# Two transformer-like blocks in one kernel: in the wide chunks, the 512-column and 256-column matmuls of a group no longer alternate

## The chip, the cores and the metric

The kernel runs on one core of one Trainium2 chip. TensorE does the matrix products, VectorE, ScalarE and GpSimd do the elementwise work, and SyncE issues the weight transfers. The metric is the device time of one execution in microseconds, as the median over runs.

## The reference

The input is 256 tokens of width 1024, in fp32. Two blocks follow one another. The first has chunked attention and a gated recurrence side by side, then a gated feed-forward part of width 2816. The second has a gated delta-rule layer and a block-sparse attention layer, each followed by a feed-forward part of width 4096 with a squared ReLU. What matters here are the feed-forward parts:

```python
    gu = hn @ w_ffn_in[l]                  # 1024 -> 2 x 2816
    g, up = jnp.split(gu, 2, axis=-1)
    h = h + (jax.nn.silu(g) * up) @ w_ffn_out[l]
...
def squared_relu_mlp(hn, w_up, w_down):    # 1024 -> 4096 -> 1024, twice
    return jnp.square(jax.nn.relu(hn @ w_up)) @ w_down
```

Every product is computed from fp32 operands at close to fp32 accuracy.

## The kernel before, in words

**Split operands.** Each fp32 operand is held as a high part and a low part, both of the reduced format fp32r. A product w x becomes wh xh + wh xl + wl xh. The weights are fetched in 170 chunks of 128 x 2048 elements (1 MB) into three slots of RAW. ScalarE writes the high part WH (line 373) and VectorE the low part WL (line 382). TensorE then multiplies the chunk. The semaphores raw_in, hi_done, lo_done and mm_done pass a slot from one to the next.

**Narrow chunks.** `product` (lines 386 to 388) issues three matmuls of 256 columns for each 128 x 128 block of weights: wh xh, wh xl and wl xh, one for each term, one column per token.

**Wide chunks.** For the up-projections of the feed-forward parts (segments fi, u0 and u1: 22 + 16 + 16 = 54 chunks), the high and low parts of the input lie side by side in XHL. One matmul of 512 columns (line 445) multiplies wh by both, into a whole PSUM bank, and one of 256 columns (line 447) adds wl xh into the upper half of that bank. A chunk has 256 output columns, that is two blocks b of 128, each in a bank of its own, and 8 blocks k of 128 input rows. So it has 16 pairs of matmuls: for b = 0 all eight k, then for b = 1. In the first chunk of a segment the input comes in four pieces of two k, and the order is piece, b, k.

**Row chunks.** The down-projections (fo, w0 and w1: 11 + 16 + 16 = 43 chunks) take 256 input rows (two k) and all 1024 output columns (eight b). All chunks of a segment add into the same eight banks. The first chunk and the last three go b by b, with both k of a bank in turn, since banks have to be taken over or handed on early; the others go k by k over all eight banks. The last two chunks of each segment are narrow (256 columns, `product`). The other 37 are wide: line 492 is the 512-column matmul and line 494 the 256-column one. The input of a row chunk is the hidden layer HHL, of the same form as XHL.

**The order of the work.** Every engine runs its own written-out order of steps, with loops over three chunks in the middle of long segments. TensorE's order is that of the source. A weight load belongs to each matmul; the source writes none of its own. A chunk begins with waits for its low part, for its bank and, in row chunks, for the hidden layer. In chunks outside the loops, small matmuls for the norm stand between the two halves of a wide chunk (`between`) or behind it.

Of the kernel before, what the change touches and what calls it, by code (L numbers as in the profile page):

```python
# [20 lines left out]
P = 128  # L21
D = 1024
TOK = 256
KB = D // P
# [4 lines left out]
KROWS = CW // D  # L29
# [100 lines left out]
def build(nc, a):  # L130
# [5 lines left out]
    def sb(name, shape, dt, kib):  # L136
        return nc.alloc_sbuf_tensor_at(name, shape, dt, offset=base + int(kib * K1) // 32 * 32)
# [11 lines left out]
    XHL = sb("XHL", [P, KB, 2, TOK], F32R, 80)  # L149
    XH, XL = XHL[:, :, 0], XHL[:, :, 1]  # L150
# [45 lines left out]
    HHL = sb("HHL", [P, 32, 2, TOK], F32R, Z + 0)  # L196
# [41 lines left out]
    vec_at, at = {}, 0  # L238
# [7 lines left out]
    with ExitStack() as ctx:  # L246
        PS = ctx.enter_context(nc.psum_tensor("PS", [P, 8, 512], F32))
# [136 lines left out]
        def product(pe, out, wh, wl, xh, xl, start, stop):  # L384

            pe.matmul(out, wh, xh, start=start, stop=False, skip_group_check=True)  # L386
            pe.matmul(out, wh, xl, start=False, stop=False, skip_group_check=True)  # L387
            return pe.matmul(out, wl, xh, start=False, stop=stop, skip_group_check=True)  # L388

        def bank_free(pe, st):  # L390
            if st.i is not None or st.base >= SLOTS:
                pe.wait_ge(freed[st.slot], st.uses(-SLOTS))

        def order_of(pieces):

            if pieces is None:
                return [(b, k) for b in range(2) for k in range(KB)]
            return [(b, k) for p in range(0, KB, 2) for b in range(2) for k in (p, p + 1)]
# [26 lines left out]
        def wide_banks(st):  # L425
            return PS[:, WIDE[st.j % SLOTS]:WIDE[st.j % SLOTS] + 2, :]
# [5 lines left out]
        def multiply_wide(pe, st, pieces=None, between=None):  # L432

            pe.wait_ge(lo_done, st.count())
            bank_free(pe, st)
            h = WH[:, st.slot].rearrange("p (k n) -> p k n", k=KB)
            l = WL[:, st.slot].rearrange("p (k n) -> p k n", k=KB)
            for n, (b, k) in enumerate(order_of(pieces)):
                if n == KB and between:
                    between()  # L440
                if pieces is not None and b == 0 and k % 2 == 0:
                    pe.wait_ge(pieces[0], pieces[1] + k // 2 + 1)
                out = wide_banks(st)[:, b]
                part = slice(b * P, b * P + P)
                pe.matmul(out, h[:, k, part], XHL[:, k].rearrange("p e t -> p (e t)"), start=(k == 0), stop=False,  # L445
                          skip_group_check=True)
                mm = pe.matmul(out[:, TOK:512], l[:, k, part], XH[:, k], start=False, stop=(k == KB - 1),  # L447
                               skip_group_check=True)
            mm.then_inc(mm_done, 1)

        def product_t(pe, out, xh, xl, wh, wl, start, stop):
# [4 lines left out]
        ROW_BANK = (0, 1, 2, 3, 6, 7, 4, 5)  # L456

        def wide_bank_read(pe, wide, bank_):

            c = max(wide.first + j for j in range(wide.n) if WIDE[j % SLOTS] == bank_)  # L460
            pe.wait_ge(freed[c % SLOTS], c // SLOTS + 1)
# [6 lines left out]
        def multiply_rows(pe, st, ready, wide):  # L468

            pe.wait_ge(lo_done, st.count())  # L470
            pe.wait_ge(s_.hl_done, ready)
            h = WH[:, st.slot].rearrange("p (k n) -> p k n", k=KROWS)
            l = WL[:, st.slot].rearrange("p (k n) -> p k n", k=KROWS)
            left = st.seg.n - st.j if st.i is None else None
            first = st.i is None and st.j == 0
            order = [(k, b) for k in range(KROWS) for b in range(KB)]
            if first or left in (1, 2, 3):
                order = [(k, b) for b in range(KB) for k in range(KROWS)]
            for k, b in order:
                at = bass.ds(st.rel * KROWS + k, 1)  # L480
                xhl = HHL[:, at].rearrange("p k e t -> p (k e t)")
                xh, xl = xhl[:, 0:TOK], xhl[:, TOK:512]
                part = slice(b * P, b * P + P)
                out = PS[:, ROW_BANK[b]]
                if first and k == 0 and b in (0, 2, 4, 6):
                    wide_bank_read(pe, wide, (2, 2, 6, 4)[b // 2])
                if left == 2 and k == 0 and b % 2 == 0:
                    pe.wait_ge(s_.low_added, 4 * (row_no[st.seg.name] - 1) + b // 2 + 1)
                if left in (1, 2):
                    mm = product(pe, out[:, 0:TOK], h[:, k, part], l[:, k, part], xh, xl, False, left == 1 and k == KROWS - 1)  # L490
                else:
                    pe.matmul(out, h[:, k, part], xhl, start=first and k == 0, stop=False,  # L492
                              skip_group_check=True)
                    mm = pe.matmul(out[:, TOK:512], l[:, k, part], xh, start=False, stop=left == 3 and k == KROWS - 1,  # L494
                                   skip_group_check=True)
                if left == 3 and b % 2 and k == KROWS - 1 and b < KB - 1:
                    mm.then_inc(s_.low_rows, 1)
                if left == 1 and b < KB - 1 and k == KROWS - 1 and (b % 2 or st.seg.name == "w1" and b == KB - 2):
                    mm.then_inc(s_.rows_done, 1)
            mm.then_inc(mm_done, 1)  # L500

# [1365 lines left out]
        def _(pe):  # L1867
# [10 lines left out]
            def times_x_wide(m):  # L1878

                def body(st):  # L1880
                    if st.i is not None:
                        return multiply_wide(pe, st)
                    multiply_wide(pe, st, None if st.j else (s_.xl_ready, 4 * m),
                                  between=lambda: norm_point(pe, m, 2 * st.j))
                    norm_point(pe, m, 2 * st.j + 1)
                return body
# [41 lines left out]
            steps(pe, seg["wo"], lambda st: multiply(pe, st, OH, OL, (s_.ml_done, 0) if st.j == 0 else None))  # L1928
            steps(pe, seg["fi"], times_x_wide(1), head=3)
            steps(pe, seg["fo"], lambda st: multiply_rows(pe, st, st.local(0, 2), seg["fi"]), head=1, tail=SLOTS)  # L1930

            def four(b):
# [193 lines left out]
            def mlp(layer):  # L2126
                steps(pe, seg[f"u{layer}"], times_x_wide(3 + 2 * layer), head=3)
                w = seg[f"w{layer}"]
                steps(pe, w, lambda st: multiply_rows(pe, st, st.local(HBASE[f"u{layer}"]), seg[f"u{layer}"]), head=1, tail=SLOTS)
# [68 lines left out]
```

## Time and profile before

| | |
|---|---|
| median of 3 runs | 1126.56 us (1125.75 to 1126.63) |
| profiled execution | 1126.75 us |
| its span, first to last instruction | 1125.0 us |
| granted TensorE clock, mean | 0.998 |
| TensorE busy | 1112.1 us, 99% |
| VectorE busy | 765.5 us, 68% |
| ScalarE busy | 589.9 us, 52% |
| mean transfer rate | 166 GB/s over the span |

Busy time is what an engine spent inside instructions. For TensorE it is not a measure of its peak: matmul records overlap, and their ends are modelled. The interval between two starts is what a stream of matmuls costs. A row of a timeline begins with the start in microseconds from the start of the span, and then has the duration.

### The profile page before, as it was taken

How to read it: one execution, taken by the hardware profiler on the slowest of the kernel's cores; microseconds unless marked ns; L12 is line 12 of the kernel's file. 1: busy time of each engine (PE TensorE's matmuls, PEld its weight loads, DVE VectorE, ACT ScalarE, POOL GpSimd, SP SyncE). 2: the span in 40 equal slices, each digit the busy share in tenths (PEclk: the TensorE clock that was granted, in tenths of full speed). 3: DMA queues.
4: the chain of work that ended last, by engine and by line, in shares of the span. 5: the costliest groups of instructions: out<-in, count | busy, mean ns of one | idle time of the engine just before them, and what ended most of it. 6: DMA issues, size and time to landing. Idle time of an engine off the chain costs nothing.

```text
span 1125.0 us, 19980 instructions
## 1 busy us (share of the span) xinstructions
PE 1112.1 (99%) x7954; PEld 1037.1 (92%) x7954; DVE 765.5 (68%) x943; ACT 589.9 (52%) x791; POOL 218.3 (19%) x216
## 2 busy tenths in 40 slices
PE   8999999999999999999999999999999999999997
PEld 8999999999888889999999988888899999888887
DVE  6656985666877754699886777764467657876443
ACT  6547557535655543665664556643354445665332
POOL 2995003302000000167844010000030002000000
PEclk9999999999999999999999999999999999999999
DMA  9774442655655555446410356555545444655541
GB/s 296 214 229 150 150 140 93 224 181 175 200 186 186 186 192 188 145 149 188 150 39 2 112 164 197 195 192 186 187 150 188 151 145 148 198 191 214 188 149 38
DMA packets 154994, 187.31 MB, mean 166 GB/s; under 512 B 6544, under 2 KB 143920, under 8 KB 154928
## 3 DMA queue, kind: packets, MB, share of 16 engines
q1 hardware_dynamic: 151360, 184.06, 50.2%
q10 hardware_dynamic: 3568, 2.31, 0.7%
q8 instruction: 48, 0.79, 0.3%
q14 instruction: 18, 0.15, 0.0%
HBM read 185.29 MB, written 1.07 MB: 166 GB/s over the span
## 4 chain that ended last, share of the span: by engine, by line
PE 87%; POOL 5%; DVE 5%; issue 1%; ACT 1%; DMA 0%; DVEq 0%; SPq 0%; POOLq 0%; ACTq 0%
PE PS L445 18%; PE PS L492 12%; PE PS L386 10%; PE PS L387 9%; PE PS L388 9%; PE PS L447 9%; PE PS L494 6%; POOL XN L910 2%; DVE WL L382 2%; POOL XN L905 1%; POOL TAP L908 1%; PE PS L453 1%; PE PS L452 1%; PE PS L454 1%; PE PS L2012 1%; PE PS L2025 1%
## 5 line engine op out<-in xcount | busy, mean ns | idle before, releaser
L382 DVE TENSOR_TENSOR WL<-RAW,WH 128x2048 fp32r<-128x2048 f32 x170 | 399.5, 2352 | 213.1 <-ACT WH L373 213.0
L373 ACT ACTIVATE WH<-RAW 128x2048 fp32r<-128x2048 f32 x170 | 325.0, 1912 | 219.1 <-PE PS L494 121.1
L445 PE MATMUL PS<-XHL,WH 128*128 128x512 f32 x864 | 300.9, 395 | 0.0
L386 PE MATMUL PS<-XHL,WH 128*128 128x256 f32 x832 | 239.9, 288 | 3.6 <-DVE WL L333 2.4
L447 PE MATMUL PS<-XHL,WL 128*128 128x256 f32 x864 | 239.7, 277 | 0.0
L388 PE MATMUL PS<-XHL,WL 128*128 128x256 f32 x832 | 235.4, 283 | 0.0
L387 PE MATMUL PS<-XHL,WH 128*128 128x256 f32 x832 | 235.4, 283 | 0.0
L492 PE MATMUL PS<-HHL,WH 128*128 (+1 forms) x592 | 205.4, 394 | 0.0
L445 PEld LDWEIGHTS PS<-XHL,WH 128*128 128x128 f32 x864 | 162.1, 188 | 37.5
L386 PEld LDWEIGHTS PS<-XHL,WH 128*128 128x128 f32 x832 | 159.5, 192 | 7.2 <-issue 2.8
L494 PE MATMUL PS<-HHL,WL 128*128 (+1 forms) x592 | 164.0, 277 | 0.0
L447 PEld LDWEIGHTS PS<-XHL,WL 128*128 128x128 f32 x864 | 162.4, 188 | 0.0
L387 PEld LDWEIGHTS PS<-XHL,WH 128*128 128x128 f32 x832 | 159.6, 192 | 0.3
L388 PEld LDWEIGHTS PS<-XHL,WL 128*128 128x128 f32 x832 | 159.4, 192 | 0.0
L492 PEld LDWEIGHTS PS<-HHL,WH 128*128 128x128 f32 x592 | 111.0, 188 | 25.8
L494 PEld LDWEIGHTS PS<-HHL,WL 128*128 128x128 f32 x592 | 111.1, 188 | 0.0
L1058 ACT ACTIVATE SG<-PS 128x512 f32<-128x512 f32 x54 | 32.3, 598 | 107.7 <-PE PS L447 107.7
L580 POOL TENSOR_TENSOR XN<-XN 128x512 f32<-128x512 f32 x4 | 7.7, 1918 | 351.8 <-ACT XN L541 351.8
L1063 DVE TENSOR_TENSOR SG<-SG,PS 128x512 f32<-128x512 f32 x54 | 37.1, 687 | 30.3 <-ACT SG L1058 30.0
L386 PE MATMUL PS<-OH,WH 128*128 128x256 f32 x192 | 54.5, 284 | 0.0
L388 PE MATMUL PS<-OH,WL 128*128 128x256 f32 x192 | 54.4, 283 | 0.0
L387 PE MATMUL PS<-OL,WH 128*128 128x256 f32 x192 | 54.4, 283 | 0.0
(310 smaller groups left out, 1669.7 us busy)
## 6 DMA issues: line engine op xcount, KB each, us to landing
RAW<-in_mlp_w_up SPq DMA_DIRECT2D x32, 1024.0 KB, 5.4
RAW<-in_mlp_w_down SPq DMA_DIRECT2D x32, 1024.0 KB, 5.0
RAW<-in_w_in SPq DMA_DIRECT2D x25, 1024.0 KB, 5.2
RAW<-in_w_ffn_in_pairs SPq DMA_DIRECT2D x22, 1024.0 KB, 5.1
RAW<-in_dn_w_in SPq DMA_DIRECT2D x16, 1024.0 KB, 5.8
RAW<-in_mb_w_in SPq DMA_DIRECT2D x12, 1024.0 KB, 5.1
RAW<-in_w_ffn_out SPq DMA_DIRECT2D x11, 1024.0 KB, 4.9
RAW<-in_w_attn_out SPq DMA_DIRECT2D x4, 1024.0 KB, 5.7
```

Source lines behind the costliest of these rows:

```text
L373: act.activation(WH[:, k], RAW[:, k], ACT.Copy).then_inc(hi_done, 1)
L382: dve.tensor_tensor(WL[:, k], RAW[:, k], WH[:, k].bitcast(F32), ALU.subtract).then_inc(lo_done, 1)
L386: pe.matmul(out, wh, xh, start=start, stop=False, skip_group_check=True)
L387: pe.matmul(out, wh, xl, start=False, stop=False, skip_group_check=True)
L388: return pe.matmul(out, wl, xh, start=False, stop=stop, skip_group_check=True)
L445: pe.matmul(out, h[:, k, part], XHL[:, k].rearrange("p e t -> p (e t)"), start=(k == 0), stop=False, skip_group_check=True)
L447: mm = pe.matmul(out[:, TOK:512], l[:, k, part], XH[:, k], start=False, stop=(k == KB - 1), skip_group_check=True)
L492: pe.matmul(out, h[:, k, part], xhl, start=first and k == 0, stop=False, skip_group_check=True)
L494: mm = pe.matmul(out[:, TOK:512], l[:, k, part], xh, start=False, stop=left == 3 and k == KROWS - 1, skip_group_check=True)
L910: ins = pool.tensor_tensor(XN[:, j], XN[:, j], TAP[:, 0], ALU.add)
L1058: act.activation(two(SG[:, st.slot]), wide_sides(st)[1], ACT.Copy).then_inc(s_.low_out, 1)
L1063: dve.tensor_tensor(two(SG[:, st.slot]), two(SG[:, st.slot]), wide_sides(st)[0], ALU.add).then_inc(freed[st.slot], 1)
```

## The change

Inside a group of matmuls that share an output block, or in the k-by-k row chunks a token block, the 512-column matmuls are issued first and then the 256-column ones. A group is: in a wide chunk the eight k of one b (two k in the first chunk of a segment, which gets its input in pieces); in a row chunk the eight b of one k, or, in the first chunk of a segment and the third-last one, the two k of one b. Narrow chunks keep their order, in `multiply` and in the last two row chunks. The waits stand ahead of the same groups as before, and the semaphores are raised by the last 256-column matmul of the same groups.

```diff
@@ -435,17 +435,23 @@
-            for n, (b, k) in enumerate(order_of(pieces)):
-                if n == KB and between:
+            runs = [[(b, k) for k in range(KB)] for b in range(2)]
+            if pieces is not None:
+                runs = [[(b, k) for k in (p, p + 1)] for p in range(0, KB, 2) for b in range(2)]
+            for n, run in enumerate(runs):
+                if pieces is None and n == 1 and between or pieces is not None and n == 4 and between:
                     between()
-                if pieces is not None and b == 0 and k % 2 == 0:
-                    pe.wait_ge(pieces[0], pieces[1] + k // 2 + 1)
+                b = run[0][0]
+                if pieces is not None and b == 0:
+                    pe.wait_ge(pieces[0], pieces[1] + n // 2 + 1)
                 out = wide_banks(st)[:, b]
                 part = slice(b * P, b * P + P)
-                pe.matmul(out, h[:, k, part], XHL[:, k].rearrange("p e t -> p (e t)"), start=(k == 0), stop=False,
-                          skip_group_check=True)
-                mm = pe.matmul(out[:, TOK:512], l[:, k, part], XH[:, k], start=False, stop=(k == KB - 1),
-                               skip_group_check=True)
+                for _, k in run:
+                    pe.matmul(out, h[:, k, part], XHL[:, k].rearrange("p e t -> p (e t)"), start=(k == 0), stop=False,
+                              skip_group_check=True)
+                for _, k in run:
+                    mm = pe.matmul(out[:, TOK:512], l[:, k, part], XH[:, k], start=False, stop=(k == KB - 1),
+                                   skip_group_check=True)
             mm.then_inc(mm_done, 1)
...
-            order = [(k, b) for k in range(KROWS) for b in range(KB)]
-            if first or left in (1, 2, 3):
-                order = [(k, b) for b in range(KB) for k in range(KROWS)]
-            for k, b in order:
...
+            runs = [[(k, b) for b in range(KB)] for k in range(KROWS)]
+            if narrow or first or left == 3:
+                runs = [[(k, b) for k in range(KROWS)] for b in range(KB)]
+            for run in runs:
...
+                for k, b in run:
+                    part = slice(b * P, b * P + P)
+                    xhl, xh, xl = operands(k)
+                    if narrow:
+                        mm = product(pe, PS[:, ROW_BANK[b], 0:TOK], h[:, k, part], l[:, k, part], xh, xl, False,
+                                     left == 1 and k == KROWS - 1)
+                    else:
+                        pe.matmul(PS[:, ROW_BANK[b]], h[:, k, part], xhl, start=first and k == 0, stop=False, skip_group_check=True)
+                for k, b in [] if narrow else run:
+                    mm = pe.matmul(PS[:, ROW_BANK[b], TOK:512], l[:, k, b * P:b * P + P], operands(k)[1], start=False,
+                                   stop=left == 3 and k == KROWS - 1, skip_group_check=True)
+                if left == 3 and b % 2 and b < KB - 1:
                     mm.then_inc(s_.low_rows, 1)
```

TensorE, the head of the loop over wide chunks in segment fi, before the change (XHL is the input, WH and WL the weights' parts; a REGISTER_ALU row computes an address or a count):

```order
L107 UNCONDITIONAL_BRANCH
L107 ISA
L392 REGISTER_ALU
L445 MATMUL PS<-XHL,WH 128x512
L447 MATMUL PS<-XHL,WL 128x256
L445 MATMUL PS<-XHL,WH 128x512
L447 MATMUL PS<-XHL,WL 128x256
```

And at the same place with the change:

```order
L107 UNCONDITIONAL_BRANCH
L107 ISA
L392 REGISTER_ALU
L450 MATMUL PS<-XHL,WH 128x512 x8
L453 MATMUL PS<-XHL,WL 128x256 x8
L450 MATMUL PS<-XHL,WH 128x512 x8
L453 MATMUL PS<-XHL,WL 128x256 x8
```

The sixteen pairs of a chunk have become two runs of eight and eight; the four matmul rows shown of before are an eighth of them.

TensorE, a k-by-k row chunk at the head of the loop in segment fo, where one token block k ends and the next begins, before the change (HHL is the hidden layer; the ISA row at L492 computes the address of a token block):

```order
L492 MATMUL PS<-HHL,WH 128x512
L494 MATMUL PS<-HHL,WL 128x256
L492 ISA
L492 MATMUL PS<-HHL,WH 128x512
L494 MATMUL PS<-HHL,WL 128x256
```

And the whole chunk with the change:

```order
L505 ISA
L505 MATMUL PS<-HHL,WH 128x512 x8
L507 MATMUL PS<-HHL,WL 128x256 x8
L505 ISA
L505 MATMUL PS<-HHL,WH 128x512 x8
L507 MATMUL PS<-HHL,WL 128x256 x8
```

Each token block keeps its one address instruction, ahead of its first matmul.

## Rows read from the trace of the kernel before

**Rows 1.** The page, part 1: busy time, share of the span, instructions.
```profile
PE 1112.1 (99%) x7954; PEld 1037.1 (92%) x7954; DVE 765.5 (68%) x943; ACT 589.9 (52%) x791; POOL 218.3 (19%) x216
```

**Rows 2.** Waits, whole span: engine, line, waited for, us in total, times, longest.
```profile
ACT WH L373 <- PE PS L494: 121.1, 36, 3.7
...
PE PS L386 <- DVE WL L333: 2.4, 2, 1.4
```

**Rows 3.** Busy time in the three stretches with 512-column matmuls; clock, DMA share, GB/s.
```profile
270.27:443.05 172.78, 172.78 (x1001) 151.07 (x999) 119.83 (x126) 88.06 (x103) 5.44 (x3) 1.00 0.56 189
648.26:815.37 167.11, 167.11 (x968) 146.08 (x966) 104.01 (x85) 83.63 (x82) 5.41 (x3) 1.00 0.57 189
936.57:1103.68 167.11, 167.11 (x967) 146.09 (x966) 104.04 (x85) 84.92 (x83) 5.44 (x3) 1.00 0.53 176
sum 507.00, PE 507.00 PEld 443.24 DVE 327.89 ACT 256.61 POOL 16.29; mean PE 169.00 PEld 147.75 DVE 109.30 ACT 85.54 POOL 5.43
```

**Rows 4.** The page, part 5: the pairs' matmuls; busy us, mean ns, idle before.
```profile
L445 PE MATMUL PS<-XHL,WH 128*128 128x512 f32 x864 | 300.9, 395 | 0.0
...
L447 PE MATMUL PS<-XHL,WL 128*128 128x256 f32 x864 | 239.7, 277 | 0.0
...
L492 PE MATMUL PS<-HHL,WH 128*128 (+1 forms) x592 | 205.4, 394 | 0.0
...
L494 PE MATMUL PS<-HHL,WL 128*128 (+1 forms) x592 | 164.0, 277 | 0.0
```

**Rows 5.** Timeline of TensorE in an up-projection chunk: start us, duration us.
```profile
660.52 0.40 PE L445 MATMUL PS<-XHL,WH 128*128 128x512 f32 x1
660.75 0.28 PE L447 MATMUL PS<-XHL,WL 128*128 128x256 f32 x1
660.87 0.39 PE L445 MATMUL PS<-XHL,WH 128*128 128x512 f32 x1
...
663.88 0.27 PE L447 MATMUL PS<-XHL,WL 128*128 128x256 f32 x1
663.99 0.40 PE L445 MATMUL PS<-XHL,WH 128*128 128x512 f32 x1
```

**Rows 6.** Timeline of TensorE in a row chunk, six pairs.
```profile
419.82 0.40 PE L492 MATMUL PS<-HHL,WH 128*128 x1
...
421.90 0.40 PE L492 MATMUL PS<-HHL,WH 128*128 x1
```

**Rows 7.** Timeline of TensorE in a narrow chunk, 41 intervals.
```profile
482.00 0.28 PE L386 MATMUL PS<-XHL,WH 128*128 128x256 f32 x1
...
486.92 0.28 PE L388 MATMUL PS<-XHL,WL 128*128 128x256 f32 x1
```

**Rows 8.** Plain fp32 matmuls: groups by line, then merged timeline rows.
```profile
L1906 PE MATMUL PS<-XN,WRI 128*128 128x256 f32 x32 | 8.3, 382 | 0.3 <-POOL XN L910 0.3
...
L1958 PE MATMUL PS<-WBA,H 128*128 128x128 f32 x32 | 3.7, 275 | 0.0
...
77.41 1.03 PE L1906 MATMUL PS<-XN,WRI 128*128 128x256 f32 x4
...
470.06 3.74 PE L1958 MATMUL PS<-WBA,H 128*128 128x128 f32 x32
```

**Rows 9.** Timeline of TensorE where a pair follows two short plain matmuls.
```profile
659.96 0.38 PE L627 MATMUL PS<-IDENT,RC 128*128 128x128 f32 x2
...
660.10 0.47 PE L445 MATMUL PS<-XHL,WH 128*128 128x512 f32 x1
660.41 0.27 PE L447 MATMUL PS<-XHL,WL 128*128 128x256 f32 x1
```

**Rows 10.** Timeline of the weight loads (PEld) beside rows 5.
```profile
660.41 0.19 PEld L445 LDWEIGHTS PS<-XHL,WH 128*128 128x128 f32 x1
660.52 0.19 PEld L447 LDWEIGHTS PS<-XHL,WL 128*128 128x128 f32 x1
```

More of the change, by code:

```diff
@@ L475, in multiply_rows @@
             first = st.i is None and st.j == 0
-            order = [(k, b) for k in range(KROWS) for b in range(KB)]
-            if first or left in (1, 2, 3):
-                order = [(k, b) for b in range(KB) for k in range(KROWS)]
-            for k, b in order:
[L480 to L485, printed above, removed]
+            narrow = left in (1, 2)
@@ L486, in multiply_rows, with operands @@
+            def operands(k):
+                xhl = HHL[:, bass.ds(st.rel * KROWS + k, 1)].rearrange("p k e t -> p (k e t)")
+                return xhl, xhl[:, 0:TOK], xhl[:, TOK:512]
+            runs = [[(k, b) for b in range(KB)] for k in range(KROWS)]
+            if narrow or first or left == 3:
+                runs = [[(k, b) for k in range(KROWS)] for b in range(KB)]
+            for run in runs:
+                b = run[0][1]
+                if first and b % 2 == 0:
                     wide_bank_read(pe, wide, (2, 2, 6, 4)[b // 2])
-                if left == 2 and k == 0 and b % 2 == 0:
+                if left == 2 and b % 2 == 0:
@@ L488, in multiply_rows @@
                     pe.wait_ge(s_.low_added, 4 * (row_no[st.seg.name] - 1) + b // 2 + 1)
[L489 to L495, printed above, removed]
@@ L496, in multiply_rows @@
-                if left == 3 and b % 2 and k == KROWS - 1 and b < KB - 1:
+                for k, b in run:
[6 more added lines that the diff above has]
+                        pe.matmul(PS[:, ROW_BANK[b]], h[:, k, part], xhl, start=first and k == 0, stop=False, skip_group_check=True)
@@ L497, in multiply_rows @@
+                for k, b in [] if narrow else run:
+                    mm = pe.matmul(PS[:, ROW_BANK[b], TOK:512], l[:, k, b * P:b * P + P], operands(k)[1], start=False,
+                                   stop=left == 3 and k == KROWS - 1, skip_group_check=True)
+                if left == 3 and b % 2 and b < KB - 1:
                     mm.then_inc(s_.low_rows, 1)
-                if left == 1 and b < KB - 1 and k == KROWS - 1 and (b % 2 or st.seg.name == "w1" and b == KB - 2):
+                if left == 1 and b < KB - 1 and (b % 2 or st.seg.name == "w1" and b == KB - 2):
```

## The prediction

> **What bounds the kernel now.** I read the engine totals of the page first. TensorE is busy 99% of the span, VectorE 68% and ScalarE 52% [rows 1]. A busy TensorE need not be at its peak, so the waits come next. TensorE's longest wait for another engine is 2.4 us in all, while ScalarE alone stands 121.1 us waiting for the last matmul of a row chunk [rows 2]. The others wait for TensorE, not TensorE for them. Third, the busy table by stage, over the three stretches in which the 512-column matmuls run: 172.78 + 167.11 + 167.11 = 507.00 us, TensorE busy in all of it, at a granted clock of 1.00, which is the 2.4 GHz level; VectorE is busy 327.89 us of it and ScalarE 256.61 [rows 3]. So in these 507 us the time is the number of matmuls times the interval at which they start. An interval saved or added there reaches the end in full.
>
> The costliest groups give the counts: 864 + 592 = 1456 pairs of one 512-column and one 256-column matmul [rows 4]. Their "mean ns" (395 and 277) is not the interval: the records overlap, and their ends are modelled. The interval comes from the starts in the timeline. In an up-projection chunk ten pairs lie between 660.52 and 663.99 us: 3.47 / 10 = 0.347 us a pair. Inside a pair the 256-column matmul starts 0.23 us after the 512-column one, and the next pair 0.12 or 0.11 us later; over the ten pairs these steps sum to 2.31 and 1.16 us, 0.231 and 0.116 each [rows 5]. In a row chunk six pairs lie between 419.82 and 421.90: 2.08 / 6 = 0.347 us, though each pair there goes to another bank [rows 6]. Times 1456 that is 505 us, which fills the 507.
>
> **The change part by part.** It removes no matmul, no weight load, no wait and no DMA. Both places shown of the order have the same multiset: sixteen 512-column and sixteen 256-column matmuls a chunk, and in the loop the register instruction before each token block (the "ISA" rows) still stands once per block. Semaphores are raised by the last 256-column matmul of a bank group or chunk, which is last in both orders. Banks become free, and slots become free for ScalarE's split, at the same point of a chunk. So ScalarE, VectorE and the DMA queue are asked for the same things at the same points. None of their instructions moves, and I price all of this at 0.
>
> What moves is who stands next to whom on TensorE. Chunks in runs of eight: 51 wide chunks (864 / 16 = 54, less the three that take their input in pieces) and 31 row chunks (592 / 16 = 37, less a first and a third-last one in each of three segments). Each has two groups of 8, together 82 x 2 = 164 groups. The nine other chunks have 8 groups of 2, together 72. In a group of 8, seven 512-column matmuls now follow another of their kind, and seven 256-column ones too; in a group of 2, one of each. That makes 164 x 7 + 72 = 1220 places of each kind. The question is what an interval costs at those places.
>
> **Term 1, 256 after 256.** The three-term chunks are streams of such matmuls, each with its own weight load, from the same kind of tiles: 41 intervals between 482.00 and 486.92 us, 4.92 / 41 = 0.120 us [rows 7]. In the pairs the same interval reads 0.116. I take 0.120. Below, a stream of 128-column plain matmuls, also one weight load each, goes at (3.74 - 0.275) / 31 = 0.112 [rows 8]; nothing in the trace goes above 0.120 with 256 columns in a stream.
>
> **Term 2, 512 after 512.** The trace never has this. From below: the plain 256-column matmuls of the gates, four records in 1.03 us, less the mean 0.382 of the last, give 0.65 / 3 = 0.217 [rows 8]. From above: twice a 256-column interval, 0.240, if the cost goes by columns alone. Between them I use two equations. Suppose an interval is a + c x columns, whoever the neighbour is. The stream gives a + 256c = 0.120, the pair gives 2a + 768c = 0.3467. Then c = 0.1067 / 256 = 0.417 ns and a = 13.3 ns. Nothing forced c to come out as one column per tick of the granted 2.4 GHz clock (0.4167), and it does. I read this as: columns stream at the clock, and each matmul brings a fixed 13 ns with its weight load. That gives a 512-column interval of 0.2267 and a 256-column one of 0.120, in any order.
>
> The split inside a pair (0.231 and 0.116) is then a shift of 4 ns of the recorded start, not of the cost. That recorded starts shift is seen elsewhere: behind two short plain matmuls a 512-column one is recorded at 660.10 and its 256-column partner at 660.41, 0.31 later instead of 0.23 [rows 9]. The weight loads agree with "one a matmul, one ahead": the load for the next 512-column matmul starts at 660.41, with the 256-column matmul, and the load for the following 256-column one at 660.52 [rows 10, 5]. Grouping gives no load more or less to hide beside.
>
> Sum: 1220 x (0.2267 + 0.120 - 0.3467) = 0. The profiled execution took 1126.75 us (span 1125.0 and 1.75 around it), 0.19 above the median of the three runs, 1126.56. I predict 1126.6. Bounds for the range: both low ends, 1220 x (0.217 + 0.112 - 0.347) = -22 us; both high ends, 1220 x (0.240 + 0.120 - 0.347) = +16 us. I take 0 because the additive form uses the nearest rows, of the same number format.
>
> The Trainium skill, TensorE: Matmul & The Clock Gate, section Back-to-back issue gap, gives an isolated interval of N/2.4 + 2.5 ns at the high clock: 216 ns for 512 columns and 109 for 256. The trace does not agree: by it a pair would take 325 ns and it takes 347, and 256 columns take 120.
>
> **Rivals.** (A) Slower: the recorded split is real. A 512-column matmul costs 0.231 whatever precedes it, because the whole weight load that runs beside it disturbs it; a 256-column one costs 0.116 only when a 512-column one ran before and had its own weights in place with time to spare, and 0.120 in a stream. The place is the seven later 256-column matmuls of each group. The price is 1220 x 0.004 = +4.9 us: 1131.6. It decides from the first grouped chunk at 270 us. For it: every interval in the three-term chunks is 0.12, and two records in each pair show the split. Against it: the sum of a pair would meet the additive value only by chance, and recorded starts shift.
>
> (B) Faster: the extra over bare streaming in the 512-column matmul is a cost of changing kind (0.231 against the 0.217 of the plain stream), and a stream of its own kind is rid of it. Then 512 after 512 takes 0.217 and 256 after 256 takes 0.120, together 0.337: 1220 x -0.010 = -12 us, 1115. TensorE would stay the bound: VectorE at 327.89 of 495 us is far from it. For it: plain streams with a weight load each show only 4 to 5 ns over two ticks a column (0.217 against 0.2133, 0.112 against 0.1067). Against it: the 256-column stream changes no kind and still carries 13 ns.
>
> The skill's figure of 216 ns for 512 columns would be this rival's price; no row here shows it for this kind of matmul.
>
> (C) The change does not do what it says, since TensorE starts matmuls in an order of its own. Against it: the two kinds take turns in the timeline as in the source [rows 5]. It would give no change, 1126.6, and is counted with the forecast.
>
> **How the numbers follow.** Forecast with C 0.60, A and anything else on its side 0.21, B and anything on its side 0.19. Two tenths of a per cent, 2.3 us, is about what a measurement of this kernel can tell from no change; over 1220 places that is 1.8 ns. The forecast's own range is 1124.3 to 1128.9. The range for 8 in 10 takes in A whole and part of the way to B: 1118 to 1134. Beyond it lie B at full price and the upper bound of term 2. Faster 0.19, within 0.60, slower 0.21.
>
> **What would show it.** In the profile after, eight 512-column starts in a row should be 0.227 apart and eight 256-column starts 0.120, and the three stretches should sum to 507 us again. With 0.231 and 0.120, A is right; with 0.217 or near it, B. ScalarE's and VectorE's waits for TensorE should stay as they are. The prediction is wrong if the cost of a matmul depends on its neighbour, which the additive form excludes and no row of before tests for 512 columns.

## The result, and the profile after

The changed kernel takes 1129.4 us (median of 7 runs, 1128.72 to 1130.24), against 1126.56 for the kernel before beside it (7 runs). The ratio is 1.0028, 95% interval 1.0019 to 1.0037: 2.8 us slower. The forecast of no change was off by a little more than the 0.2% that I had called its bound; the time lies inside the range. Its profiled execution took 1130.2 us, with a span of 1128.5.

The busy table over the same three stretches, first to last matmul of the pairs (columns as in [rows 3]: stretch, its length, then TensorE, weight loads, VectorE, ScalarE and GpSimd busy, clock, DMA share, GB/s):

```profile
270.61:444.43 173.82, 173.82 (x1000) 152.89 (x999) 119.87 (x127) 88.01 (x103) 5.43 (x3) 1.00 0.57 187
649.65:817.77 168.12, 168.12 (x968) 147.87 (x966) 104.09 (x85) 83.60 (x82) 5.43 (x3) 1.00 0.57 188
939.00:1107.12 168.12, 168.12 (x968) 147.88 (x966) 104.08 (x85) 84.89 (x83) 5.43 (x3) 1.00 0.53 175
sum 510.06, PE 510.06 PEld 448.65 DVE 328.04 ACT 256.50 POOL 16.29; mean PE 170.02 PEld 149.55 DVE 109.35 ACT 85.50 POOL 5.43
```

Each stretch is 1.0 us longer than in [rows 3], 3.06 in all. The medians differ by 2.84 us. The two profiled executions differ by 3.45, of which 0.33 lies ahead of the first stretch (it begins at 270.61 instead of 270.27), where the code is the same. VectorE's and ScalarE's busy times and the clock have not moved. The waits (who waited for whom, us in total, times, longest) answer [rows 2]:

```profile
ACT WH L373 <- PE PS L507: 122.5, 36, 3.7
...
PE PS L386 <- DVE WL L333: 1.5, 1, 1.5
```

TensorE waits for nobody more than before. So the 3 us are in the intervals of its own stream. This is a wide chunk of the changed kernel on TensorE's timeline. Like matmuls are merged into one row, which gives the start of the first, the time to the end of the last, and the count:

```profile
700.59 2.00 PE L450 MATMUL PS<-XHL,WH 128*128 128x512 f32 x8
702.43 1.12 PE L453 MATMUL PS<-XHL,WL 128*128 128x256 f32 x8
703.39 0.40 PE L450 MATMUL PS<-XHL,WH 128*128 128x512 f32 x1
```

A view that starts inside the same run shows its last three:

```profile
701.75 0.84 PE L450 MATMUL PS<-XHL,WH 128*128 128x512 f32 x3
702.43 0.40 PE L453 MATMUL PS<-XHL,WL 128*128 128x256 f32 x2
```

The last three 512-column intervals take (702.43 - 701.75) / 3 = 0.227 us each, and the eight 256-column ones 0.96 / 8 = 0.120: both terms of the additive form (an interval is 13.3 ns and 0.4167 ns a column, whoever the neighbour is). But the first five take (701.75 - 700.59) / 5 = 0.232. The trace holds each start to the nanosecond, finer than the views print it; all figures in ns below are differences of such starts. A group reads

```
512 columns: 233 236 228 233 231 226 227 227   (1841; 8 x 226.7 = 1813)
256 columns: 113 119 120 120 120 120 120 120   ( 952; 8 x 120   =  960)
```

A run of 512-column matmuls behind 256-column ones pays 28 ns before it settles, and the way down gives 7 to 8 back: +20 ns a group. Both kinds of chunk show the same numbers, the wide ones with one bank a group and the row ones with eight.

The starts every 16 pairs give the time of a chunk. In segment u0, before and after, in ns:

```
chunk            first wide, 2nd, 3rd    further wide    first row   further row (twelve)
before           5650  6187  5630        5547            5547        5547
changed          5573  6174  5680        5587            5573        5587
```

The second and third hold the norm's small matmuls too. Two groups of 20 ns make the +40 of a chunk. In u0 that is 13 x 40 in the wide chunks and 12 x 40 in the row chunks; the first and the third-last row chunk, in groups of two, add 26 each, the second -13 and the third +50, and the first wide chunk gives 77 back: +1.0 us. The three segments together make 3.07 (the first has one chunk more).

### The profile page after: what moved, and what is told of

It reads as the page before. It is cut to its first block, busy times and chain, and to the rows that moved or that the text cites. A ratio compares the mean times of both kernels' runs of the same rounds, so it can differ in the third digit from the quotient of the medians.

```text
span 1128.5 us, 19980 instructions
## 1 busy us (share of the span) xinstructions
PE 1116.4 (99%) x7954; PEld 1043.9 (93%) x7954; DVE 765.7 (68%) x943; ACT 589.7 (52%) x791; POOL 217.9 (19%) x216
## 4 chain that ended last, share of the span: by engine, by line
PE 87%; POOL 5%; DVE 5%; issue 1%; ACT 1%; DMA 0%; DVEq 0%; POOLq 0%; ACTq 0%
PE PS L450 18%; PE PS L505 12%; PE PS L386 10%; PE PS L387 9%; PE PS L388 9%; PE PS L453 9%; PE PS L507 6%; POOL XN L923 2%; DVE WL L382 2%; POOL XN L918 1%; POOL TAP L921 1%; PE PS L459 1%; PE PS L458 1%; PE PS L460 1%; PE PS L2025 1%; PE PS L2038 1%
## 5 line engine op out<-in xcount | busy, mean ns | idle before, releaser
L388 PE MATMUL PS<-XHL,WL 128*128 128x256 f32 x832 | 235.9, 283 | 0.0
L450 PE MATMUL PS<-XHL,WH 128*128 128x512 f32 x864 | 220.0, 393 | 0.0
L450 PEld LDWEIGHTS PS<-XHL,WH 128*128 128x128 f32 x864 | 154.0, 189 | 26.2
L386 PEld LDWEIGHTS PS<-XHL,WH 128*128 128x128 f32 x832 | 160.1, 192 | 6.3 <-issue 2.8
L387 PEld LDWEIGHTS PS<-XHL,WH 128*128 128x128 f32 x832 | 160.2, 193 | 0.3
L388 PEld LDWEIGHTS PS<-XHL,WL 128*128 128x128 f32 x832 | 160.0, 192 | 0.0
L505 PE MATMUL PS<-HHL,WH 128*128 (+1 forms) x592 | 154.3, 393 | 0.0
L453 PEld LDWEIGHTS PS<-XHL,WL 128*128 128x128 f32 x864 | 120.3, 190 | 10.1
L453 PE MATMUL PS<-XHL,WL 128*128 128x256 f32 x864 | 123.2, 282 | 0.0
L505 PEld LDWEIGHTS PS<-HHL,WH 128*128 128x128 f32 x592 | 103.8, 189 | 16.0
L507 PEld LDWEIGHTS PS<-HHL,WL 128*128 128x128 f32 x592 | 85.7, 190 | 9.1
L507 PE MATMUL PS<-HHL,WL 128*128 (+1 forms) x592 | 88.0, 282 | 0.0
```

Of the source, the lines that this page charges most:

```text
L505: pe.matmul(PS[:, ROW_BANK[b]], h[:, k, part], xhl, start=first and k == 0, stop=False, skip_group_check=True)
L507: mm = pe.matmul(PS[:, ROW_BANK[b], TOK:512], l[:, k, b * P:b * P + P], operands(k)[1], start=False, stop=left == 3 and k == KROWS - 1, sk ...
```

## The experiments

Ratios are against the kernel before, run beside each. "Stretches" is the sum from the first to the last start of the pairs, 506.9 us before and 509.9 in the changed kernel. The first kernels set two theories against each other: S, a settling at each change from 256 to 512 columns, and N, a fixed price for each matmul behind one of its own kind.

**e1_group16**

```diff
                 for _, k in run:
                     pe.matmul(out, h[:, k, part], XHL[:, k]..., start=(k == 0), stop=False, ...)
-                for _, k in run:
+                if pieces is None and n == 0:
+                    continue
+                for b, k in run if pieces is not None else runs[0] + runs[1]:
                     mm = pe.matmul(...)
...
+                if not narrow and len(run) == KB and run[0][0] == 0:
+                    continue
+                low = run if len(run) == KROWS else runs[0] + runs[1]
```

> Runs of sixteen: in a wide chunk the sixteen 512-column matmuls of both output blocks, then the sixteen 256-column ones; in a k-by-k row chunk those of both token blocks. The first chunk of a segment and the third-last one keep their groups of two. Theory S (settling): in the changed kernel a run of 512-column matmuls behind 256-column ones starts with 233, 236, 228, 233, 231 ns and is then at 227, and the 256-column run gives 7 ns back; that is +20 ns a group, whatever its length beyond five. 82 groups instead of 164 make the three stretches 508.3 us (before 506.9, changed kernel 510.0), +0.12% over before, and the second half of each run is at 227. Theory N (a fixed price of 2.5 ns for each matmul that follows its own kind, from 3.07 us over 1220 places): 1302 places, +3.3 us, 510.2 us, +0.29%, with no drift along a run.

Measured: 1130.1 us, 1.0036 (1.0022 to 1.0049), stretches 510.7. TensorE's timeline inside one chunk, from a view that starts inside the run of 512-column matmuls:

```profile
701.58 2.43 PE L450 MATMUL PS<-XHL,WH 128*128 128x512 f32 x10
703.85 0.28 PE L455 MATMUL PS<-XHL,WL 128*128 128x256 f32 x1
```

The last ten take 2.27 / 10 = 0.227 each, so the run settles once and stays settled, as S has it. A chunk takes 5567 ns, 20 over the 5547 of before, where the changed kernel has 40. Yet the total is over what S wanted. The waits name the reason (here and in the changed kernel):

```profile
PE PS L626 <- POOL XN L604: 2.2, 4, 0.7
```

```profile
PE PS L621 <- POOL XN L599: 0.7, 1, 0.7
```

The small matmuls of the norm stand between the halves of the second chunk of a segment. Eight 256-column matmuls, 0.96 us of cover, had moved behind them, and GpSimd's sum was not ready. That chunk grew from 6174 to 6933 ns, three times: 2.3 us. (The table counts only 1.5 us more wait, since it starts from modelled ends.) My expectation had not looked at what the moved matmuls had covered.

**e5_group16_kept_norm**

```diff
-                if pieces is None and n == 0:
+                whole = pieces is None and between is None
+                if whole and n == 0:
                     continue
-                for b, k in run if pieces is not None else runs[0] + runs[1]:
+                for b, k in runs[0] + runs[1] if whole else run:
```

> e1_group16 came out at 510.7 us for the three stretches, above both theories, though its runs of sixteen looked as theory S wants them; one start in the second chunk of each segment was 0.65 us late, on the small matmul of the norm, which the first eight 256-column matmuls no longer stood ahead of. Here only the chunks without such norm matmuls get runs of sixteen (45 wide ones, 31 row ones); the rest is as in the changed kernel. Theory S: 20 ns less in each of the 76 chunks, 510.0 - 1.5 = 508.4 us, +0.13% over before. Theory N: 1220 + 76 places, 510.1 us, +0.28%. The wait of e1 should be gone from TensorE's waits.

Measured: 1128.11 us, 1.0016 (1.0006 to 1.0025), stretches 508.5, chunks 5567. That is S. N's 510.1 is out.

**e2_group4** (and **e3_group2** with GROUP = 2)

```diff
-                for _, k in run:
-                    pe.matmul(out, h[:, k, part], ...)
-                for _, k in run:
-                    mm = pe.matmul(out[:, TOK:512], ...)
+                for g in range(0, len(run), GROUP):
+                    for _, k in run[g:g + GROUP]:
+                        pe.matmul(out, h[:, k, part], ...)
+                    for _, k in run[g:g + GROUP]:
+                        mm = pe.matmul(out[:, TOK:512], ...)
```

> Groups of four where the changed kernel has groups of eight. Theory S: each group pays nearly the whole settling, 233+236+228+233 then 113.5+119+120+120 = 1402.5 ns against 1386.7 for four alternating pairs, +15.8 ns in each of 328 groups: +5.2 us, the three stretches at 512.1 us, +0.46% over before, so slower than groups of eight. Theory N: 1056 like-neighbour places at 2.5 ns, +2.7 us, 509.5 us, +0.24%, so faster than groups of eight.

> Groups of two everywhere. Theory S, from the chunks of the changed kernel that are in groups of two: 233+236+116+112+233+230+114+119 = 1393 ns for two groups against 1386.7, +3.2 ns in each of 728 groups: +2.3 us, +0.2% over before. Theory N: 728 places at 2.5 ns, +1.8 us, +0.16%. The two are close here; the run shows whether the cost has its maximum at a length between two and sixteen, which S wants and N does not.

Measured: groups of four 1131.47 us, 1.0045 (1.0031 to 1.0058), stretches 512.0 where S said 512.1. Groups of two 1128.54 us, 1.0019 (1.0010 to 1.0028), stretches 508.9, between S's 509.2 and N's 508.7, so this run alone does not tell the two apart. Groups of four on TensorE's timeline:

```profile
699.95 1.09 PE L452 MATMUL PS<-XHL,WH 128*128 128x512 f32 x4
700.88 0.64 PE L455 MATMUL PS<-XHL,WL 128*128 128x256 f32 x4
701.36 1.09 PE L452 MATMUL PS<-XHL,WH 128*128 128x512 f32 x4
702.29 0.63 PE L455 MATMUL PS<-XHL,WL 128*128 128x256 f32 x4
```

Each run of four takes 0.93, that is 0.2325 a matmul; none settles at 0.227. Of the lengths tried, four costs the most, which a price by neighbours cannot give.

**e4_all512**

```diff
-                    mm = pe.matmul(out[:, TOK:512], l[:, k, part], XH[:, k], start=False, ...)
+                    mm = pe.matmul(out, l[:, k, part], XHL[:, k].rearrange("p e t -> p (e t)"), start=False, ...)
...
-                    mm = pe.matmul(PS[:, ROW_BANK[b], TOK:512], l[...], operands(k)[1], start=False,
+                    mm = pe.matmul(PS[:, ROW_BANK[b]], l[...], operands(k)[0], start=False,
```

> The low weights' matmul of every pair of the changed kernel is widened from 256 to 512 columns (it then also adds the product of the two low parts, in the lower half of the bank), so that there is no change of size inside a wide or row chunk. The additive form of the prediction (13.3 ns + 0.4167 ns a column, 0.2267 us for 512 columns) gives 1456 x 2 x 0.2267 = 660.1 us for the pairs, +155.3 us over before, 1281.9 us in all. Rival A's term (0.231 for 512 columns whatever the neighbour) gives 1456 x 2 x 0.231 = 672.7, +168 us, 1294. Twice a 256-column interval, 0.240, gives +194 us, 1320. Rival B's 0.217 gives +127 us, 1253.

Measured: 1281.02 us, 1.1373 (1.1355 to 1.1390), stretches 661.6. Additive said 1281.9; rival A's term is 13 us off, rival B's 28. Only at the head of a segment, behind 256-column matmuls, do the first starts run 233, 236, 228, 233 and 230 ns apart, as S has it. From the fourth chunk on they are 226.7 ns apart throughout (again merged), (802.97 - 801.16) / 8 = 0.226:

```profile
801.16 1.98 PE L453 MATMUL PS<-XHL,WL 128*128 128x512 f32 x8
802.97 0.39 PE L450 MATMUL PS<-XHL,WH 128*128 128x512 f32 x1
```

Chunks take 7253 ns, and 32 x 226.7 = 7253. A stream of one size obeys the additive form; the mixture does so only in one of the orders tried, taking turns, and not always there, as the next run shows.

**e7_first_chunk_grouped**

```diff
+                if pieces is not None:
+                    if k % 2 == 0:
+                        for q in (k, k + 1):
+                            pe.matmul(out, h[:, q, part], XHL[:, q]..., start=(q == 0), stop=False, ...)
+                        pe.matmul(out[:, TOK:512], l[:, k, part], XH[:, k], ...)
+                    else:
+                        mm = pe.matmul(out[:, TOK:512], l[:, k, part], XH[:, k], ...)
+                    continue
```

> The kernel before, with the 512-column matmuls in groups of two in the first wide chunk of each segment alone (3 of 54 chunks); all others take turns. In the trace of before that chunk and half of the next run at 353.3 ns a pair instead of 346.7, and return to 346.7 behind the small norm matmuls. In the changed kernel the same chunk in groups of two takes 5573 ns instead of 5650. If the 353.3 ns cycle is a state that lasts until something breaks it, groups of two break it at once: 77 ns less in the chunk and up to 53 ns in the next, 0.2 to 0.4 us in all, 506.5 us for the stretches, in the time no difference from before that can be measured. If it belongs to the place (the pieces, the first bank), the next chunk's first half stays at 353.3.

Measured: 1135.43 us, 1.0080 (1.0066 to 1.0094), stretches 515.8. The expectation failed in all but the first chunk, and this run taught most. The first chunk took 5573 ns, as expected. But behind it, where the code is that of before, the second and third took 6234 and 5731 ns instead of 6187 and 5630, and from the fourth to the end of each segment every chunk took 5649 to 5661 instead of 5547. Nine pairs from its row for 699.68 us on:

```profile
699.68 0.40 PE L455 MATMUL PS<-XHL,WH 128*128 128x512 f32 x1
...
700.74 0.40 PE L455 MATMUL PS<-XHL,WH 128*128 128x512 f32 x1
...
701.80 0.40 PE L455 MATMUL PS<-XHL,WH 128*128 128x512 f32 x1
...
702.86 0.40 PE L455 MATMUL PS<-XHL,WH 128*128 128x512 f32 x1
```

Three pairs take 1.06 us, 0.353 each. The kernel before has this too, in its first chunk and a half of each segment:

```profile
273.80 0.40 PE L445 MATMUL PS<-XHL,WH 128*128 128x512 f32 x1
...
274.86 0.40 PE L445 MATMUL PS<-XHL,WH 128*128 128x512 f32 x1
...
276.98 0.40 PE L445 MATMUL PS<-XHL,WH 128*128 128x512 f32 x1
```

Taking turns has two cycles, with these single intervals in ns, 512 and 256 columns in turn:

```
one:    231+112 233+117              346.7 a pair, 5547 a chunk
other:  233+117 241+120 236+113      353.3 a pair, 5653 a chunk
```

In every trace here each lasts until other matmuls come between. Which one it is was decided by what stood ahead, not by the stream. Nor was it where the later code lies in the program: e7 has as many matmuls as the kernel before (7954 records on TensorE in both), and they differ only in their order in the first chunk of each segment.

**e8_wide_only**: the wide part of the change alone.

```diff
-            for n, (b, k) in enumerate(order_of(pieces)):
+            for n, run in enumerate(runs):
...    (multiply_wide as in the changed kernel, multiply_rows as before)
```

> Only the wide chunks are grouped, the row chunks take turns. Theory S and N alike put 51 x 40 ns = 2.0 us here, less the gain of the three first chunks, and 31 x 40 ns = 1.2 us in the row chunks: stretches at 508.7 us, +0.16%. If banks mattered (one bank for a whole group in wide chunks, eight banks in row chunks), the share would be another one: nothing here and all in the rows, or the other way round.

Measured: 1131.72 us, 1.0047 (1.0033 to 1.0060), stretches 512.5 where 508.7 was expected: slower than the whole change. The wide chunks took 5587 as expected, but the row chunks, left as before, 5649 to 5661. They run in the slow cycle from the first one on; what they follow, grouped chunks instead of alternating ones, is the only change of order.

**e9_wide_only_two_ahead**

```diff
+                if first and k == 0 and b == 0:
+                    for _ in range(2):
+                        pe.matmul(out[:, 0:P], ONES[:], ONES[:], start=True, stop=True)
```

> e8_wide_only with two plain 128-column fp32 matmuls ahead of the first row chunk of each segment, into a bank that the first real matmul then starts anew. In e8 the row chunks, whose code is that of before, took 5653 ns instead of 5547: taking turns has two cycles, 346.7 and 353.3 ns a pair, and the one it falls into lasts. Theory C (cycles): what matters is what stands ahead of the stream; two small matmuls ahead can put the 31 + 6 row chunks into the 346.7 ns cycle, as the norm's do in the kernel before: stretches at about 512.5 - 37 x 0.107 + 1 = 509.6 us, 1129.2 in all. They need not: in e7_first_chunk_grouped the norm's matmuls did not bring it there. If the rows stay at 5653 the time is that of e8 plus 1 us, 1132.7. Rival: row chunks are slow because of what the grouped wide chunks did to the banks or to the other engines' timing; then they stay at 5653 whatever stands ahead.

Measured: 1129.72 us, 1.0028 (1.0017 to 1.0038), stretches 509.9. Two more matmuls ahead of the row chunks of each segment make the kernel 2 us faster (2.6 in the stretches). TensorE's timeline shows the four records they leave, and then, in a later row chunk, seven pairs:

```profile
739.97 0.61 PE L495 MATMUL PS<-ONES 128*128 128x128 f32 x4
...
779.94 0.39 PE L501 MATMUL PS<-HHL,WH 128*128 x1
...
782.37 0.40 PE L501 MATMUL PS<-HHL,WH 128*128 x1
```

2.43 / 7 = 0.347. From the third row chunk on each takes 5547. The code of these chunks, the data and the wide chunks ahead are those of e8, so the rival that the expectation names (banks, or the other engines' timing) is out.

**e10_before_two_ahead**

```diff
+            if pieces is not None:
+                for _ in range(2):
+                    pe.matmul(wide_banks(st)[:, 0, 0:P], ONES[:], ONES[:], start=True, stop=True)
```

> The kernel before with the same two plain matmuls ahead of the first wide chunk of each segment. Theory C: the 24 pairs that run at 353.3 ns there may fall into the 346.7 ns cycle at once (-0.16 us a segment, +0.3 for the two matmuls: no change that can be measured, 1126.9), and then the norm's matmuls meet another phase and can leave all that follows in the 353.3 ns cycle: 3 x 29 x 0.107 = +9.3 us, 1135.5, as in e7. It is one of these two, not a value between, if the cycles are all there is. Theory N (price by neighbours) has no change here, +0.3 us.

Measured: 1136.08 us, 1.0084 (1.0070 to 1.0098), stretches 515.7 (516.8 with the two spare matmuls ahead of each): the second branch. The first 24 pairs did fall into the fast cycle (the first two chunks take 5636 and 6133 ns, before 5650 and 6187). Everything behind the last of the norm's small matmuls, from the third chunk on, runs at 353.3. Six pairs there:

```profile
699.84 0.40 PE L448 MATMUL PS<-XHL,WH 128*128 128x512 f32 x1
...
700.90 0.40 PE L448 MATMUL PS<-XHL,WH 128*128 128x512 f32 x1
...
701.96 0.40 PE L448 MATMUL PS<-XHL,WH 128*128 128x512 f32 x1
```

From row to row it is three pairs, 1.06 us. Two harmless matmuls at the head of each of the three segments cost 10 us in all.

**e11_rows_only**: `multiply_rows` as in the changed kernel, `multiply_wide` as before.

```diff
-            for k, b in order:
+            for run in runs:
...    (multiply_rows as in the changed kernel)
```

> Only the row chunks are grouped; the wide chunks take turns as before. The wide chunks stay in the 346.7 ns cycle, since nothing ahead of them differs from before: 5547 ns from the third on. The row chunks in groups of eight take 5587 each: 31 x 0.040 = +1.2 us, stretches at 508.1 us, 1127.7, +0.11%. A value near e8's +5 us would say that grouping either part costs the other its fast cycle.

Measured: 1127.71 us, 1.0011 (1.0002 to 1.0020), stretches 508.2: as expected. The parts alone cost 1.3 us (rows) and 5.6 us (wide), the whole 3.1. The parts do not add, because the grouped rows took 5587 ns behind either kind of wide chunk, and the rows that take turns did not keep their 5547.

**e6_low384_grouped** and **e12_low384_alternating**

```diff
-    ... pe.matmul(out[:, TOK:512], l[:, k, part], XH[:, k], ...)
+    ... pe.matmul(out[:, 0:384], l[:, k, part], XHL[:, k].rearrange("p e t -> p (e t)")[:, 0:384], ...)
...    (in the row chunks likewise)
```

> The changed kernel with the low weights' matmul widened from 256 to 384 columns (it then also adds low times low for half the tokens). Additive form: 13.3 + 0.4167 x 384 = 173.3 ns, a pair 400 ns, a chunk 6400 ns, 1456 x 0.400 = 582.4 us, +77.7 us over before, 1204.2 us. Theory of size (the settling belongs to any change from shorter to longer matmuls): a settling shows here as well, a chunk of two groups stands 20 to 40 ns above 6400. Theory of the loads (it belongs to 256-column streams, whose weight loads, 192 ns long in the record and 120 apart, follow each other without a gap): with 384 columns the loads are 173 ns apart, and a chunk takes 6400 ns with 512-column starts at 227 from the first.

> The kernel before, taking turns, with the low weights' matmul at 384 columns (it also adds low times low for half the tokens). e6_low384_grouped had 6533 ns a chunk, 133 over the additive 6400, with weight loads 175 ns apart: so the settling there does not need back-to-back loads of a 256-column stream, and its 512-column runs never came to 227. If taking turns has a cycle at the additive value here too, 6400 ns a chunk, the stretches take 582 us and the whole 1202; if it runs in a slower cycle, between 6400 and 6700, up to 1229.

Measured: grouped 1216.05 us, 1.0796 (1.0779 to 1.0812), 6533 ns a chunk; taking turns 1213.8 us, 1.0778 (1.0761 to 1.0794), 6507 a chunk. The additive form wants 6400 in both. So with 512 and 384 columns the mixture costs 107 ns a chunk even where it takes turns. In the grouped one the 512-column intervals are 229, 233, 236, 224, 231, 236, 228 and 233 ns, none of them 227; the eight 384-column ones ahead of them take (701.55 - 700.13) / 8 = 0.1775 instead of 0.1733:

```profile
700.13 1.58 PE L453 MATMUL PS<-XHL,WL 128*128 128x384 f32 x8
701.55 2.01 PE L450 MATMUL PS<-XHL,WH 128*128 128x512 f32 x8
```

Neither theory had this: size said 20 to 40 ns a chunk over 6400, the loads none, and it was 133. The number that stood for the loads (6400) has failed, but their part is not settled by it, since the edit did not pull them apart. These are two neighbouring weight loads in the run of 384-column matmuls, from one timeline each:

```profile
700.48 0.19 PEld L453 LDWEIGHTS PS<-XHL,WL 128*128 128x128 f32 x1
```

```profile
700.66 0.19 PEld L453 LDWEIGHTS PS<-XHL,WL 128*128 128x128 f32 x1
```

In that run the loads start 173 to 185 ns apart and their records last 188: they still follow each other without a gap. In e4 the loads start 227 ns apart and have a gap between them, and the stream is even; but all sizes are equal there too, so it does not tell the two theories apart.

All orders of the same sixteen pairs, as ns a chunk in the steady state: taking turns 5547 in the one cycle and 5653 in the other, runs of sixteen 5567, of two 5573, of eight 5587, of four 5613. No order tried went below 5547, which is 16 x (226.7 + 120), and no kernel was built to beat the one before. What the slow cycle costs it is 6.7 ns in each of the 24 pairs at the head of a segment, 0.5 us in all.

## Why the prediction was right and wrong

**Bound: right.** The 3.06 us of the stretches are the difference of the medians (2.84) to within the spread of the runs. TensorE's waits and the other engines' busy times did not move.

**No work added, releases at the same points: right.** No engine waits longer for another. In e1, which went one step further, the cover of the moved matmuls did count; the change itself had left it in place.

**Term 1, 256 after 256 at 0.120: right.** Once settled, it is 0.120.

**Term 2, 512 after 512 at 0.2267: right as the settled value, wrong as the mean over the 1220 places.** In a group of eight the places after the first average about 230. The lower bound of 0.217 was read from records, and there are two records to one plain matmul (the four records of e9 are two matmuls), so it is the interval of half a matmul; the forecast did not use it. e4 confirms the form itself by the clock on the wall: 1281.0 against 1281.9.

**The step that failed** is "That gives a 512-column interval of 0.2267 and a 256-column one of 0.120, in any order". I solved for two unknowns from a pure stream and an alternating one and took the clean slope as proof that the neighbour does not matter. But neither stream had one 512-column matmul behind another, so they could not show it, and the alternating one has the additive value only in one of its two cycles. The order matters by +20 ns for a settled group, and by +6.7 ns a pair between two cycles of one and the same order. The second was in the trace of before, in the first 24 pairs of each segment. I took my ten pairs at 660 us and the six at 420, both from the fast cycle, and did not compare chunk times along a segment: 5650 stood there beside 5547. That comparison would have shown before any run that what stands ahead changes an interval, and put more chance on slower.

**Luck.** That the change came out so near to nothing rests on the cycle that the kernel before happened to be in. Against the slow cycle, at 5653 ns a chunk, groups of eight at 5587 would save 66 ns a chunk: the changed kernel at 1129.4 us is 6.7 us faster than e10, which differs from the kernel before by six small matmuls. The forecast had no term for this.

**The shift of recorded starts** (231 to 233 and 112 to 117 ns in turn) was read rightly as no cost of its own: the pair sums to the additive value. But these steps also tell one cycle from the other (the slow one has 241 + 120 in it), and I had explained them away.

**Rival A** came true in its sign, by luck: it said +4.9 us against 3.06 measured, from 256-column matmuls at 0.120 and 512-column ones at 0.231 for ever. The trace has 0.227 in every settled run, and runs of sixteen cost less than runs of eight, against it. **Rival B** is out: no chunk came below the additive value, e4 included. The Trainium skill, TensorE: Matmul & The Clock Gate, section Back-to-back issue gap, has 216 ns for an isolated interval of 512 columns. The stream of e4, in which each matmul loads its weights, does not agree: 226.7. **Rival C** is out: the timeline shows runs of eight.

**What stays open** is what the state is. Two small matmuls ahead can set it (e9, e10). The same +40 ns a chunk came with one bank a group and with eight, and for both input tiles; e9 against e8 speaks against the other engines; the granted clock was 1.00 in these stretches in both kernels, and in e7 and e10, so it does not explain the difference, but no run varied it. That weight loads without a gap between them have a part in it is neither shown nor ruled out. It would take loads that are pulled apart, in a mixture of sizes, to tell. What in TensorE holds the state, and why 384 columns have no cycle at the additive value, no run here tells.

## What to carry to other kernels

Where TensorE streams matmuls of two sizes, each with its own weights, measure the time per repetition along the whole segment, not in one place: the same code can run in a fast and in a slow cycle (346.7 and 353.3 ns a pair here), chosen by what stands ahead. A small edit far ahead, even two spare matmuls a segment, can then move the total (up by 0.8% in e10, down by 0.2% from e8 to e9), so an edit's effect is judged by the chunk times on both sides of it. Long runs of one size were not the fastest order here, but they took the same time behind every entry tried; where matmuls are moved, ask what they had been covering.

## What the hardware showed that I had not expected

- One order of the same matmuls has two lasting rates. e10 against before: 5653 against 5547 ns a chunk, 1136.1 against 1126.4 us, with two small matmuls a segment as the only difference.
- Two extra matmuls a segment made a kernel faster: e9 against e8, 1129.7 against 1131.7 us.
- Cost does not rise or fall steadily with the length of a run: +0 (fast cycle), +27, +67, +40 and +20 ns a chunk for runs of 1, 2, 4, 8 and 16.
- A 512-column fp32r matmul with its own weight load settles at 226.7 ns and a 256-column one at 120.0: 13.3 ns over one column per tick at 2.4 GHz, for both (e4, and the changed kernel's runs).
